# Moving the large SBUF regions to a common byte offset, and reading the filler products from other offsets

## The reference, cut to what matters

```python
h = modulate(rms_norm(x, norm1_g[l]), sh1, sc1)
qa, ka, va, qb, kb, vb, ga, gb = split_in_proj(h @ w_in[l])
x = x + gt1 * merge_branches(ya, yb, ga, gb, w_proj_a[l], w_proj_b[l], w_out[l])
h2 = modulate(rms_norm(x, norm2_g[l]), sh2, sc2)
x = x + gt2 * swiglu(h2, w_ffn_gate[l], w_ffn_up[l], w_ffn_down[l])
...
# second block
h = rms_norm_2(x, norm_gain)
y_a = (nsa_mixer(...) * silu(g_nsa)) @ w_proj_a
y_b = (rglru_mixer(...) * silu(g_lru)) @ w_proj_b
x = x + (sigmoid(gate_a) * y_a + sigmoid(gate_b) * y_b) @ w_out
```

## Time and profile before

| | us |
|---|---|
| median of 3 runs | 2462.16 |
| lowest, highest | 2461.98, 2464.65 |
| span of the profiled execution, first to last instruction | 2459.3 |
| TensorE busy in it | 2379.4 (97%) |
| VectorE, ScalarE busy | 1547.7, 1129.1 |
| mean granted TensorE clock | 0.992 of full speed |

### The profile page before, as it was taken

The page is one execution under the profiler, slowest core; times in us unless marked ns, Lnnn a source line. Parts: engine busy times, 40 slices in busy tenths (PEclk is TensorE's granted clock), DMA queues, the critical chain, the costliest instruction groups (busy, mean ns, idle before and its releaser), DMA issues.

```text
span 2459.3 us, 32774 instructions
## 1 busy us (share of the span) xinstructions
PE 2379.4 (97%) x12351; PEld 1990.5 (81%) x12351; DVE 1547.7 (63%) x2398; ACT 1129.1 (46%) x1785; POOL 165.6 (7%) x292
## 2 busy tenths in 40 slices
PE   7999999999999999999999999999999999999898
PEld 3888877788888888888878877897888877877687
DVE  5786777788676554454686777754333367389763
ACT  5647777723321121122547777333222355467541
POOL 0200000110000000000100000100000010011020
PEclk9999999999999999999999999999999999999999
DMA  7421111363433333322221111522222334521263
GB/s 283 148 74 45 52 40 46 114 240 121 154 122 136 120 125 132 120 86 78 103 85 58 48 48 64 180 86 97 92 95 94 103 101 138 183 88 64 85 205 103
DMA packets 68866, 267.71 MB, mean 109 GB/s; under 512 B 8576, under 2 KB 8640, under 8 KB 67696
## 3 DMA queue, kind: packets, MB, share of 16 engines
q1 hardware_dynamic: 42336, 162.94, 19.2%
q0 software_dynamic: 26384, 102.77, 12.0%
HBM read 237.37 MB, written 27.26 MB: 108 GB/s over the span
## 4 chain that ended last, share of the span: by engine, by line
PE 79%; DVE 9%; ACT 6%; issue 4%; DMA 2%; POOL 0%; SPq 0%; ACTq 0%; DVEq 0%
PE ps L190 22%; PE ps L192 22%; PE ps L191 22%; DVE w_lo L186 2%; PE ps L1235 1%; PE ps L1236 1%; PE ps L1169 1%; PE ps L1237 1%; PE ps L1176 1%; DMA ada_raw<-in_ada 1%; DVE inv L1399 1%; ACT w_hi L179 1%; PE ps L1218 1%; ACT pr L1298 1%; DVE maxes L1422 1%
## 5 line engine op out<-in xcount | busy, mean ns | idle before, releaser
L190 PE MATMUL ps<-h_hi,w_hi 128*128 128x512 f32 (+2 forms) x2104 | 751.8, 357 | 14.4 <-DVE h_lo L1538 6.3
L192 PE MATMUL ps<-h_hi,w_lo 128*128 128x512 f32 (+2 forms) x2104 | 742.5, 353 | 0.0
L191 PE MATMUL ps<-h_lo,w_hi 128*128 128x512 f32 (+2 forms) x2104 | 741.6, 352 | 0.0
L186 DVE TENSOR_TENSOR w_lo<-w_raw,w_hi 128x1024 fp32r<-128x1024 f32 x288 | 358.3, 1245 | 199.7 <-ACT w_hi L179 199.5
L190 PEld LDWEIGHTS ps<-h_hi,w_hi 128*128 128x128 f32 x2104 | 398.0, 189 | 78.2 <-issue 14.3
L192 PEld LDWEIGHTS ps<-h_hi,w_lo 128*128 128x128 f32 x2104 | 398.4, 189 | 56.9
L191 PEld LDWEIGHTS ps<-h_lo,w_hi 128*128 128x128 f32 x2104 | 398.2, 189 | 56.4 <-issue 2.4
L179 ACT ACTIVATE w_hi<-w_raw 128x1024 fp32r<-128x1024 f32 x288 | 302.8, 1052 | 297.7 <-PE ps L192 288.1
L190 PE MATMUL ps<-q_hi,w_hi 128*128 128x512 f32 x720 | 256.1, 356 | 1.4 <-DVE q_lo L1559 1.4
L192 PE MATMUL ps<-q_hi,w_lo 128*128 128x512 f32 x720 | 256.7, 356 | 0.0
L191 PE MATMUL ps<-q_lo,w_hi 128*128 128x512 f32 x720 | 256.5, 356 | 0.0
(11 more groups left out here) (373 smaller groups left out, 3452.2 us busy)
## 6 DMA issues: line engine op xcount, KB each, us to landing
w_raw<-in_stream SPq DMA_DIRECT2D x288, 512.0 KB, 3.3
wt<-in_ada_t POOLq DMA_DIRECT2D x72, 512.0 KB, 3.6
ada_raw<-in_ada SPq DMA_DIRECT2D x4, 2048.0 KB, 18.0
x_keep<-x POOLq DMA_DIRECT2D x8, 768.0 KB, 7.8
gates<-th_g POOLq DMA_DIRECT2D x16, 384.0 KB, 2.6
gates<-sg POOLq DMA_DIRECT2D x24, 256.0 KB, 2.3
wt_q<-in_ada_t POOLq DMA_DIRECT2D x8, 512.0 KB, 3.6
gates<-th_g POOLq DMA_DIRECT2D x16, 256.0 KB, 2.3
```

What stands on the lines that cost most here:

```text
L186: nc.vector.tensor_tensor(w_lo[:, u % 3, :], raw[:, u % 2, :], w_hi[:, u % 3, :].bitcast(F32), ALU.subtract).then_inc(lo_ready, 1)
L190: nc.tensor.matmul(out_ap, lh, rh, start=start, stop=False)
L191: nc.tensor.matmul(out_ap, lh, rl, start=False, stop=False)
L192: return nc.tensor.matmul(out_ap, ll, rh, start=False, stop=stop)
```

## The change

The five small tiles and the region of h are allocated after all other regions, so that every large region begins at 128 modulo 512 bytes. And `keep_awake` takes a list of places to read: the moving operand starts at other columns of the next unit's high or low weights (in bytes modulo 512, ahead of layer 1: 192 and 320, then 256, then 0 and 136; ahead of the second block: 384 and 128, then 128, then 320 and 128), and the 14 fillers of the third group before the second block take columns of w_lo at 320 as weights in place of identR. Counts of products stay, as do all sizes, loops, queues and waits.

```diff
--- before.py
+++ after.py
@@ -37,6 +37,8 @@
 
 N_QKV, N_GATE, N_MERGE, N_OUT = 12, 16, 8, 8
 FF_PARTS = (8, 8, 6)
+AWAKE = {True: ([("hi", 16, "ident", 0), ("hi", 48, "ident", 0)], [("hi", 32, "ident", 0)], [("hi", 96, "ident", 0), ("hi", 2, "ident", 0)]),
+         False: ([("hi", 64, "ident", 0), ("hi", 128, "ident", 0)], [("lo", 0, "ident", 0)], [("hi", 48, "lo", 48), ("hi", 0, "lo", 48)])}
 PER_LAYER = N_QKV + N_GATE + N_MERGE + N_OUT + sum(2 * f + CH for f in FF_PARTS)
 N_IN2 = 6 + 4 + 1 + 4 + 4 + 4 + 16
 N_CMP = 8
@@ -91,25 +93,11 @@
         cosT, sinT = r_t["cosT"], r_t["sinT"]
         band = sb("band", [P, 3 * P], F32R)
         identR = sb("identR", [P, P], F32R)
-        aff = sb("aff", [P, DEPTH, 2, CH, 2])
-        nsink = sb("nsink", [P, 16])
-        small = sb("small", [P, 16])
-        cs = sb("cs", [P, 16])
-        cs4 = sb("cs4", [P, CH, 4], F32R)
-        gains = aff[:, 0, 0, :, 0]
         r_x = region("region_x", 4 * CH * TOK,
                      [("x", [P, CH, TOK], F32)],
                      [("qa", [P, 3, TOK], F32R), ("qb", [P, 3, TOK], F32R), ("sums", [P, TOK], F32), ("inv", [P, TOK], F32)],
                      [("s_lo", [P, 2, 4, SEQ], F32R), ("bias", [P, 2, W_LEN], F32)],
                      [("a", [P, 4, SEQ], F32), ("th", [P, 4, SEQ], F32), ("aa", [P, 4, SEQ], F32)])
-        r_h = region("region_h", 8 * CH * (TOK + 2),
-                     [("h_hi", [P, CH, TOK + 2], F32R), ("h_lo", [P, CH, TOK + 2], F32R)],
-                     [("ada_raw", [P, 3, 4 * UNIT], F32)],
-                     [("h2_hi", [P, CH, SEQ], F32R), ("h2_lo", [P, CH, SEQ], F32R), ("r_hi", [P, 2, 16, 62], F32R),
-                      ("r_lo", [P, 2, 16, 62], F32R)],
-                     [("h2_below_s", [P, 2 * CH, SEQ], F32), ("s_hi", [P, 2, 4, SEQ], F32R)],
-                     [("h2_below_r", [P, 2 * CH, SEQ], F32), ("rg", [P, 4, SEQ], F32), ("ig", [P, 4, SEQ], F32)])
-
         r_q1 = region("region_q_hi", 4 * CH * TOK, [("q_hi", [P, CH, TOK], F32R)], [("qf", [P, CH, TOK], F32)],
                       [("ada_raw3", [P, 4 * UNIT], F32), ("below_band", [P, UNIT], F32), ("band_raw", [P, 3 * P], F32)], [("ada_lo3", [P, 4 * UNIT], F32R)],
                       [("y_hi", [P, CH, SEQ], F32R), ("br", [P, SEQ], F32), ("br_cols", [P, 4, 32], F32), ("kcx", [P, 2, 32], F32R),
@@ -144,6 +132,19 @@
                      [("gn", [P, 4, SEQ], F32), ("sg2", [P, 2, SEQ], F32)], [("ada_row", [4, 4, 512], F32)],
                      [("th_g", [P, 2, TOK], F32), ("es", [P, 2, TOK], F32)],
                      [("ga", [P, 2, TOK], F32), ("gb", [P, 2, TOK], F32)], [("root_row", [P, TOK], F32), ("rooted_x", [P, 4, SEQ], F32)])
+        r_h = region("region_h", 8 * CH * (TOK + 2),
+                     [("h_hi", [P, CH, TOK + 2], F32R), ("h_lo", [P, CH, TOK + 2], F32R)],
+                     [("ada_raw", [P, 3, 4 * UNIT], F32)],
+                     [("h2_hi", [P, CH, SEQ], F32R), ("h2_lo", [P, CH, SEQ], F32R), ("r_hi", [P, 2, 16, 62], F32R),
+                      ("r_lo", [P, 2, 16, 62], F32R)],
+                     [("h2_below_s", [P, 2 * CH, SEQ], F32), ("s_hi", [P, 2, 4, SEQ], F32R)],
+                     [("h2_below_r", [P, 2 * CH, SEQ], F32), ("rg", [P, 4, SEQ], F32), ("ig", [P, 4, SEQ], F32)])
+        aff = sb("aff", [P, DEPTH, 2, CH, 2])
+        nsink = sb("nsink", [P, 16])
+        small = sb("small", [P, 16])
+        cs = sb("cs", [P, 16])
+        cs4 = sb("cs4", [P, CH, 4], F32R)
+        gains = aff[:, 0, 0, :, 0]
         x, h_hi, h_lo = r_x["x"], r_h["h_hi"], r_h["h_lo"]
         ps = ctx.enter_context(nc.psum_tensor("ps", [P, 8, 512], F32))
         psf = ps[:, :, :].rearrange("p b n -> p (b n)")
@@ -484,10 +485,12 @@
                                    c == 0, c == CH - 1)
                 return mm
 
-        def keep_awake(u, count):
+        def keep_awake(u, count, *reads):
 
             for k in range(count):
-                nc.tensor.matmul(ps[:, 0, :], identR[:, :], w_hi[:, u % 3, 0:512], start=True, stop=True)
+                moving, m0, weights, w0 = reads[k * len(reads) // count]
+                tiles = {"hi": w_hi[:, u % 3, :], "lo": w_lo[:, u % 3, :], "ident": identR[:, :]}
+                nc.tensor.matmul(ps[:, 0, :], tiles[weights][:, w0:w0 + P], tiles[moving][:, m0:m0 + 512], start=True, stop=True)
 
         class Norm:
 
@@ -854,11 +857,12 @@
                 else:
                     e.wait_ge(lo_ready, base + 1)
                     e.wait_ge(before_units.sem, before_units.base + 5)
-                    keep_awake(base, 12)
+                    first, second_, third = AWAKE[stacked]
+                    keep_awake(base, 12, *first)
                     norm.statistic(e)
-                    keep_awake(base, 6)
+                    keep_awake(base, 6, *second_)
                     norm.spread(e)
-                    keep_awake(base, 14)
+                    keep_awake(base, 14, *third)
                     norm.first_units(e, base)
                 for t in range(2, T):
                     linear_tile(t)
```

## The result

The changed kernel takes 2451.13 us (median of 4, 2449.63 to 2452.88); the kernel before, run beside it, 2463.40 (median of 4, 2461.98 to 2466.80). The ratio is 0.995, with a 95% interval of 0.9936 to 0.9964: 12.3 us or 0.5% faster, where 27.2 were forecast. The value lies inside the range, near the 2451 of rival (1). The profiled execution of after took 2452.88 us, 1.75 above its median; its span is 2450.9, its mean clock 0.989 (before: 2459.3 and 0.992).

The account below looks back on a forecast made before the run. TensorE, busy for 97% of the span, was taken as the bound, with other engines' work hidden in the linears. Terms of 11.4 + 6.6 + 2.6 + 4.6 + 2.0 = 27.2 us off 2462.2 gave 2435 us, range 2418 to 2463.

Parts of the forecast that it names:

- rival (1): Steady streams come only to h2's 229.0 ns level and ragged h gains nothing: 11.6 us, so 2451; chance 0.19.
- (a): Layer 1's q and n, second block's y, all 512 wide, from 320 to 128: saves 11.4 us, or 7.3 at 229.0 ns.
- (b): Layer 0's q, 1440 products of mean width 384: excess shrinks from 13.8 to 9.2 ns, saving 6.6 us.
- (d): Ragged h, the largest group, moved by 64 bytes: half of 9.2 us taken, 4.6 us saved; bounds 0 and 20.7.
- (e): Attention, p from 320 and qa, qb from 192 to 128: 2 us saved for both layers; bounds 0 and 8.
- (c): h2, 1128 products from 192 to 128 at 2.3 ns each: 2.6 us saved; bounds 0 and 2.6.
- (f): Fillers ahead of layer 1 and the second block: slower reads covered by a wait or costing 0.1 us; zero in the sum.
- (g): VectorE, ScalarE and DMAs get other addresses: no effect, and in the linears TensorE covers it.
- the 3 allowed: Clock: short stretches at 1.2 in place of 2.4 GHz after waits may begin earlier or later, 3 us either way.
- (2): Rival: the offset modulo 512 is not the cause, so nothing changes, 2462 us; chance 0.14.
- (3): Rival: an operand's low or high place in SBUF counts, not its offset: 13.7 us slower, 2476; chance 0.12.
- (4): Rival: ragged h and attention reach their upper bounds: 49.3 us saved, 2413; chance 0.10.

Follow-up runs that it names:

- experiment 6: Changed kernel with all 512-column triples of a unit of layer 0's q ahead of all 256-column ones: 2452.57 us, ratio 0.9951.
- experiment 7: Kernel before the change, with layer 0's q grouped by width in all but the first unit: 2467.02 us, ratio 1.0013.
- experiment 8: Changed kernel with rows of h_hi and h_lo 832 numbers long in place of 770, DMA scratch 4096 bytes in place of 8192: 2441.43 us, ratio 0.9904.
- experiment 9: Changed kernel with only the DMA scratch cut from 8192 to 4096 bytes: 2447.20 us, ratio 0.9932.
- experiment 4: Changed kernel with the old fillers, which read w_hi at 128 everywhere: 2451.59 us, ratio 0.9946.
- experiment 1: Changed kernel with 192 bytes of small tiles ahead of the regions, putting them at 320 with weights at 128: 2466.14 us, ratio 1.0013.
- experiment 3: Changed kernel with the regions in their old order, but each still at 128 modulo 512: 2452.89 us, ratio 0.9954.
- experiment 2: Changed kernel with 192 bytes of small tiles ahead of w_raw, putting weights and regions all at 320: 2450.65 us, ratio 0.9945.
- experiment 5: Changed kernel with filler tiles ahead of the regions, weights at 128, in two versions: regions at 256, 2467.84 us; regions at 384, 2449.70 us.
- experiment 10: Changed kernel with rows of 832, the small scratch and q grouped by width: all units 2448.93 us, all but the first 2441.65 us.

## Why the prediction was right or wrong

**(a) Steady streams at 512 columns.** Forecast 11.4 us, measured 4.75 + 5.24 + 1.39 = 11.4. To take the fillers' 226.7 for changing weights was right; rival (1)'s 229 for them was wrong. That the weights change from product to product plays no part.

**(b) Layer 0's q: the step that failed.** The forecast was twice the measured gain, and 8.2 of the 14.9 us between them are here: forecast -6.6 us, measured +1.6. The others are 3.3 in (d), 1.7 in (e), 1.0 in (c), and 0.8 in the stretch up to 171 us, for which there was no term. The step was "the excess of 13.8 shrinks as in (a), to 13.4/20.0 of it". It took the excess for something in proportion to the columns, which would have been 6.7 ns at 256. At distance 0 it is the same 13.3 ns for either width (experiment 6), and at distance 192 a narrow product had only 11 to begin with (experiment 7): it gets dearer by the move. Even a perfectly settled stream would give (226.7 + 120.0)/2 = 173.3, half a nanosecond or 0.7 us under the 173.8 of before. And the alternating triples never settle, which turns it into a loss. A warning stood in the rows: 173.8 at a mean of 384 columns is 13.8 ns of excess, hardly more than the 13.4 that the fillers had at 512; the mixed stream was already nearly as good as the good one.

**(c) h2.** Forecast -2.6, measured -1.6 with the products between; in the steady stretch exactly the 2.3 ns forecast (229.0 to 226.7). Elsewhere the products of h2 stand in bursts of 3 to 24 among others, and these hardly moved: the burst of 24 at 2032 us gained 0.02 us, where 2.3 ns each would be 0.06.

**(d) The ragged h.** Forecast -4.6, measured -1.3, and against it the 0.4 that its first projections lost. That part of its excess comes from the 8-byte steps was right; that half was the other part was a choice between bounds, and too much. Experiment 8 gives the split for the wide ones: of the 5.4 ns that they are above 226.8 the rows' length keeps all. That these steps decide h's cost alone was on the list of what would make the forecast wrong, and it did. The upper bound of 20.7 us was wrong for the same reason as (b): it took 2.6 ns from each narrow product, where in the rows of 832 they take 120, as before. What h had to give was 5.8 us (experiment 9). A slip beside it: 258 columns in place of 256 raise the mean by one column, 0.4 ns and not 0.2; it changes no term.

**(e) Attention.** Forecast -2, measured -0.3 at most. Where its 512-wide products follow each other without a wait, they took 231.6 and 231.4 ns (layers 0 and 1) before, 232.0 and 231.5 after. That the triples over ragged h break its bursts is not enough of a reason: in experiment 8, where they are ragged no more, they take 232.6 and 230.3, and layer 0's attention is 0.3 us shorter. That the bursts are too short to settle would explain it, but is only argued.

**(f), (g) Fillers, other engines, clock.** Nothing for the fillers by the medians (experiment 4) and nothing for VectorE, as forecast. The clock moved by 3.7 us in the profiled pair, just over the 3 allowed, and against the change.

With the measured values the sum is 11.4 - 1.6 + 1.6 + 1.3 + 0.3 = 13.0, less 0.8 up to 171 us: 12.2 us, beside 12.3 between the medians. That it fits to a tenth is luck, as the runs of one kernel differ by some 3 us.

**The rivals.** (1) has the right time, 2451, by another sum: 7.3 from (a) and 4.3 from (b), where 11.4 and -1.6 were measured. Only its half on ragged h held. (2) is refuted by experiment 1, (3) by experiments 1 and 3, (4) by h at 175.4 and attention unmoved.

What was to show it: q, n, y and h2 near 227, as forecast; the unit of h near 175, 175.4; the fillers at 320 slower than at 136 only just (234 against 233), which is no more than the reading's own error; 136 is itself 8 bytes off. There was no line for layer 0's q among these signs, though it carried the second largest term.

**The rule weighed.** All offsets of experiments 1, 2, 5 and all of q's are multiples of 16 bytes, and 512 columns took 226.7, 229.0, 232.3 or 233.3 ns by distance. The Trainium skill, "SBUF — State Buffer", in its box on cachelines, knows only the crossing of 16-byte lines, by which experiments 1, 2 and the change itself would all have come out at 2462; the measurement decides, and it is not the whole rule. The Trainium skill, "TensorE: Matmul & The Clock Gate", section "Wait — 56ns, not 53.3ns?", gives a warm product a fixed 2.5 ns on top of its columns. The trace agrees with the form, a fixed amount whatever the width, but at distance 0 alone, and with 13.3 ns in place of 2.5.

## What to carry to other kernels

In a kernel bound by TensorE, place moving operands of 512 columns, row by row, at the same byte offset modulo 256 as the weights (the runs tried distances 0 and 256), and pad rows whose length would make chunks drift (here 5.8 us, half as much as all region moves together). An excess over the columns must be measured at each width before it is scaled: one at 512 columns says nothing of 256. At such an offset keep equal widths together where nothing else waits for the order (by the profiles 2 us at most, by the medians nothing, experiment 10), and leave the first unit, which follows its producer, alone; at distance 192 grouping cost 1.6 ns a product.

## What was not expected of the hardware

- The cost of a float32r product with 512 columns depends on the distance of the two operands' offsets, and is back at its start after 256 bytes: 226.7, 229.0, 232.3, 233.3, 226.7 ns at 0, 64, 128, 192, 256.
- At distance 0 the excess over the columns is 13.3 ns at 256 and at 512 columns. At 192 it is 11 and 20.
- At distance 0 a stream takes some five products after a change of width to reach its pace, 232 ns each in place of 226.7 when it goes from 256 to 512 columns.
- Chunks that lie 8 bytes further on each, within 56 bytes of the weights for h_hi, cost a 512-wide stream as much as a distance of 128 (232.2 against 232.3), wherever the region begins; fillers that are all 8 bytes off take 233.
- Halving the DMA scratch ends the program 3 us sooner behind its last store (3.9 in place of 6.9 us).

Why the offsets of two operands act together, and what the end of the program does with the scratch, these runs don't say.
